# A hybrid attention and expert layer on one core: the first 512 value columns move from the projection slots into the opening sweep

## The reference, cut to what matters

```python
ada = silu(c) @ w_ada + b_ada                     # (1, 6 * 2048), w_ada 2048 x 12288
sh_m, sc_m, gt_m, sh_f, sc_f, gt_f = split(ada, 6)
h = rms_norm(x, g_pre_mix) * (1 + sc_m) + sh_m    # x: 256 tokens x 2048
proj = h @ w_in                                   # w_in 2048 x 6160
qa, ka, va, qb, kb, vb, rb, zb = split(proj)      # 1024, 1024, 1024, 512, 512, 1024, 1024, 16 columns
oa = diff_attention(qa, ka, va, rel_bias, lam)    # 8 heads, two softmax maps each, 2 blocks of 128 queries
ob = rms_norm(gla(qb, kb, vb, log_a(zb))) * silu(rb)
x = x + gt_m * rms_norm(concat(oa, ob) @ w_out, g_post_mix)
h = rms_norm(x, g_pre_ffn) * (1 + sc_f) + sh_f
x = x + gt_f * rms_norm(hier_moe(h), g_post_ffn)  # 32 experts, w1 and w3 2048 x 512, w2 512 x 2048 each
```

## Time and profile before

| | |
|---|---|
| median of 3 runs | 1465.71 us (1464.82 to 1466.46) |
| the profiled execution | 1463.97 us, of it span 1462.0 us |
| busy shares | TensorE 84%, VectorE 53%, ScalarE 14%, GpSimd 4% |
| chain that ended last | TensorE 45%, DMA 44%, VectorE 6% |
| moved | 583.5 MB, mean 399 GB/s |

### The profile page before, as it was taken

How to read it: one execution, slowest core, us unless ns; L and a number is a source line. 1 busy time by engine, 2 the same in 40 slices (tenths; PEclk the granted TensorE clock), 3 DMA queues, 4 the chain that set the end, 5 groups by cost and what they waited for, 6 DMA issues and landing times.

```text
span 1462.0 us, 18971 instructions
## 1 busy us (share of the span) xinstructions
PE 1221.2 (84%) x7437; PEld 575.1 (39%) x7438; DVE 778.9 (53%) x1110; ACT 211.7 (14%) x491; POOL 52.9 (4%) x68
## 2 busy tenths in 40 slices
PE   4699999999999989886777677758676679999967
PEld 4578884744444443222222222212222223333322
DVE  5877487877769666342234323422333335555525
ACT  3010121232110041010000000000000001111103
POOL 1000300011100020000000000000000000000020
PEclk9899999999999999988888889987888889999989
DMA  9999988797999899999999999999999999999996
GB/s 354 392 383 384 351 317 346 291 378 274 367 409 412 345 379 396 431 430 433 431 432 431 430 434 430 430 432 432 434 431 432 431 432 431 431 432 430 433 427 262
DMA packets 81557, 583.52 MB, mean 399 GB/s; under 512 B 5280, under 2 KB 30160, under 8 KB 56816
## 3 DMA queue, kind: packets, MB, share of 16 engines
q1 hardware_dynamic: 74160, 564.41, 93.6%
q10 hardware_dynamic: 5808, 14.85, 2.7%
q0 software_dynamic: 1552, 3.75, 0.8%
HBM read 579.30 MB, written 3.69 MB: 399 GB/s over the span
## 4 chain that ended last, share of the span: by engine, by line
PE 45%; DMA 44%; DVE 6%; SPq 2%; issue 1%; ACT 1%; POOL 0%; ACTq 0%; DVEq 0%
DMA stream<-in_w 41%; PE ps L1019 9%; PE ps L788 8%; PE ps L675 5%; PE ps L1075 4%; PE ps L740 3%; DMA stream<-in_w_ada 3%; PE ps L1026 2%; PE ps L975 2%; PE ps L878 2%; PE ps L969 2%; SPq L510 2%; PE ps L785 1%; DVE stream L1298 1%; DVE wk L1161 1%; DVE acc L1270 1%
## 5 line engine op out<-in xcount | busy, mean ns | idle before, releaser
L1019 PE MATMUL ps<-stream,wk 128*32 128x512 f32 x2304 | 330.2, 711 | 179.6 <-DMA stream<-in_w 178.9
L1536 DVE TENSOR_TENSOR acc<-ps,acc 128x2048 f32<-128x2048 f32 x37 | 84.8, 2292 | 364.4 <-PE ps L975 364.4
L1019 PEld LDWEIGHTS ps<-stream,wk 128*32 128x32 f32 x2304 | 74.7, 125 | 417.5 <-issue 332.5
L788 PE MATMUL ps<-stream 128*128 128x512 f32 x320 | 140.5, 593 | 0.1
L1075 PE MATMUL ps<-stream,cst 128*32 128x512 f32 x1152 | 131.5, 595 | 8.4 <-DMA stream<-in_w 8.4
L675 PE MATMUL ps<-stream 128*128 128x256 f32 x512 | 118.1, 394 | 1.8 <-ACT stream L1681 1.8
L675 PEld LDWEIGHTS ps<-stream 128*128 128x128 f32 x512 | 100.9, 198 | 16.8 <-issue 1.9
L1026 PEld LDWEIGHTS ps<-cst,wk 128*128 128x128 f32 x576 | 76.4, 207 | 69.0 <-issue 69.0
L975 PE MATMUL ps<-wk,cst 32*128 32x512 f32 x592 | 91.1, 687 | 0.8 <-ACT wk L1876 0.8
L1161 DVE SCALAR_TENSOR_TENSOR wk<-stream,cc,wk 128x768 f32<-128x768 f32 (+1 forms) x90 | 83.6, 929 | 11.0 <-DMA stream<-in_w_ada 8.3
L788 PEld LDWEIGHTS ps<-stream 128*128 128x128 f32 x320 | 59.5, 190 | 69.7 <-issue 69.7
(11 more groups left out here) (281 smaller groups left out, 1105.4 us busy)
## 6 DMA issues: line engine op xcount, KB each, us to landing
stream<-in_w SPq DMA_DIRECT2D x87, 4096.0 KB, 41.9
stream<-in_w_ada SPq DMA_DIRECT2D x64, 1024.0 KB, 8.8
stream<-in_w_in SPq DMA_DIRECT2D x8, 4096.0 KB, 16.5
stream<-in_w SPq DMA_DIRECT2D x16, 2048.0 KB, 11.7
stream<-in_w_ada SPq DMA_DIRECT2D x64, 384.0 KB, 10.1
stream<-in_w_ada SPq DMA_DIRECT2D x16, 512.0 KB, 9.7
stream<-in_w_in SPq DMA_DIRECT2D x4, 2048.0 KB, 13.7
stream<-in_w_out SPq DMA_DIRECT2D x2, 4096.0 KB, 16.4
```

What stands on the lines that cost most here:

```text
L788: last = nc.tensor.matmul(bank(fill % 2), hT[:, k, P * half:P * half + P], w[:, k, :], start=(k == 0), stop=(k == KD - 1))
L1019: last = nc.tensor.matmul(bank(1 + m)[32 * g:32 * g + 32, :], xe[:, k + g, :], w13[m][:, k + g, :], start=(k == 0), stop=(k == KD - 4))
L1536: V.tensor_tensor(y4, ps[:, b0:b0 + 4, :], y4, ALU.add).then_inc(ysum_sb, 1)
```

## The change

The opening sweep gets two more units, 8 and 9. Each is one block of 128 tokens (t = 0 or 1) by the 512 columns 2048 to 2559: one matmul of 512 columns for each k step, with `hT` as the stationary side and the weights as the moving side. They use bank 6 too, so four units share it (`SHARED = 4`), and the running sums of the two new ones lie in `acc`; the last stage's sum goes to `va`. The weights come in further slabs of 512 columns (rows of 2 KB), after the 2048 columns of the stage. Unit 4 is gone from the slots, with its load and its seven products; 28 slots remain, unit 5 is the only block unit, and attention starts at slot 4. `ADA_IN` is written anew: four slots take one load, 22 take two, two take none, and the four steps after them are as before. The row of the relative bias is computed ahead of the sweep's last unit, in bank 7, and its two tables are loaded ahead of GpSimd's other loads. The semaphore of the three small loads at the start is one with that of the constants.

```diff
-HEADS_READY = [8, 16]
+WIDE = 10
+SHARED = WIDE - 6
-TURN = [6, 0, 1, 2, 7, 3, 4, 5]
-SLOTS = 32
-BLOCK_UNITS = [4, 5]
+TURN = [6, 0, 7, 1, 8, 2, 3, 4, 9, 5]
+ADDED_AT = {8: {1: 6, 3: 7, 5: 8}, 4: {0: 6, 2: 7, 3: 8}}
+SLOTS = 28
+BLOCK_UNITS = [5]
-ATT_FROM = 6
-ADA_IN = [1, 1, 1, 1, 1, 1, 1, 1, 2, 2, 2, 2, 0, 2, 2, 1, 2, 2, 2, 1, 2, 2, 0, 2, 1, 2, 2, 2, 3, 2, 2, 0, 4, 5, 4, 3]
+ATT_FROM = 4
+ADA_IN = [1, 1, 1, 1, 2, 2, 2, 2, 2, 2, 0, 2, 2, 2, 2, 2, 2, 2, 2, 0, 2, 2, 2, 2, 2, 2, 2, 2, 4, 5, 4, 3]
...
+def wide_slabs(j):
+    lo, hi = STAGES[j]
+    cuts = [lo] + [k for k in range(lo + 1, hi) if k % HOMES in (0, 6)] + [hi]
+    return list(zip(cuts, cuts[1:]))
...
-    out = [(4 * i + 3.9, ("unit", i + 2)) for i in range(8)]
+    out = [(4 * i + 3.9, ("unit", i + 3)) for i in range(7)]
...
+        def wide_home(lo, hi):
+            r = lo % HOMES
+            return slab(s4, 4096 + 512 * r, hi - lo, 512) if r < 6 else slab(gl, 1920 + 512 * (r - 6), hi - lo, 512)
...
+                for a_, b_ in wide_slabs(j):
+                    if a_ == 6:
+                        sp.wait_ge(xT_ps, 4 * TT)
+                    sp.dma_start(wide_home(a_, b_), w_in[:, a_:b_, 256 * EARLY:256 * EARLY + 512]).then_inc(early_w_in[j % 3], 16)
...
-                    pe.wait_ge(add_sb, 2 * j + u - HELD)
+                    pe.wait_ge(add_sb, SHARED * j + u - HELD)
+                if u >= EARLY:
+                    t = u - EARLY
+                    for k in range(lo, hi):
+                        last = nc.tensor.matmul(bank(HELD), hT[:, k, P * t:P * t + P], wide_home(k, k + 1)[:, 0, :], start=(k == lo), stop=(k == hi - 1))
+                    last.then_inc(add_ps, 1)
+                    return last
...
-                    if n == EARLY - 2 and j + 1 < len(STAGES):
+                    if n == WIDE - 2 and j + 1 < len(STAGES):
                         early_sums(j + 1)
+                    if n == WIDE - 1 and j + 1 == len(STAGES):
+                        pe.wait_ge(tab_in, 16 * len(tables))
+                        pe.wait_ge(early_mod, len(STAGES))
+                        nc.tensor.matmul(bank(7)[:, 0:SKEW], relb, bkt[:, 0:SKEW], start=True, stop=True).then_inc(relrow_ps, 1)
...
-                    if j and n_ in (len(pieces(j)) // 4, 3 * len(pieces(j)) // 4):
-                        added(j - 1, HELD + n_ // (len(pieces(j)) // 2))
+                    if j and n_ in ADDED_AT[len(pieces(j))]:
+                        added(j - 1, ADDED_AT[len(pieces(j))][n_])
...
+                if j:
+                    added(j - 1, WIDE - 1)
```

More of the change, by code:

```diff
@@ L153, in schedule @@
     beside = [[] for _ in range(SLOTS)]
-    beside[0] += [("alpha", 0), ("row",)]
+    beside[0] += [("alpha", 0)]
     beside[1] += [("alpha", 1)]
@@ L157, in schedule @@
     beside[3] += [("lam",), ("tail", 0)]
-    beside[7] += [("tail", 1)]
-    beside[4].append(("alpha", 2))
+    beside[3].append(("alpha", 2))
     for m in (2, 3):
@@ L168, in schedule @@
         beside[ATT_FROM + j].append(("att", j))
-    beside[12].append(("kdec",))
-    beside[25].append(("kv", 0))
-    beside[26] += [("glao", 0), ("kv", 1)]
-    beside[27] += [("glao", 1), ("gsq", 0)]
-    beside[28] += [("gsq", 1)]
-    beside[29] += [("gmul", 0, 0), ("gmul", 1, 0)]
-    beside[30] += [("gmul", 0, 1)]
-    beside[31] += [("glaT", 0)]
+    beside[8].append(("kdec",))
+    beside[23].append(("kv", 0))
+    beside[24] += [("glao", 0), ("kv", 1)]
+    beside[25] += [("glao", 1), ("gsq", 0)]
+    beside[26] += [("gsq", 1), ("gmul", 0, 0)]
+    beside[27] += [("gmul", 1, 0), ("gmul", 0, 1), ("glaT", 0)]
     out = []
@@ L179, in schedule @@
         i, half, part = slot_unit(s)
-        out.append(("block", i - 4, 2 * half + part) if i in BLOCK_UNITS else ("proj", i, half, part))
+        out.append(("block", i - 5, 2 * half + part) if i in BLOCK_UNITS else ("proj", i, half, part))
         out += beside[s]
@@ L198, in loads @@
 def loads():
-    out = [(4 * i + 3.9, ("unit", i + 2)) for i in range(8)]
+    out = [(4 * i + 3.9, ("unit", i + 3)) for i in range(7)]
     out += [(max(ada_slot(n - 4) + 0.5, 1.9), ("ada", n)) for n in range(4, 64)]
-    return [("unit", 0), ("unit", 1), ("ada", 0), ("ada", 1), ("ada", 2), ("ada", 3)] + [item for _, item in sorted(out)]
+    return [("unit", 1), ("unit", 2), ("ada", 0), ("ada", 1), ("ada", 2), ("ada", 3)] + [item for _, item in sorted(out)]
 def build(nc, a, out):
@@ L380, in out_block @@
         def out_block(b, t, n):
[L382 removed]
+            return va[:, t, 512 + 256 * n:512 + 256 * n + 256]
         def block_bank(b, n):
[L386 removed]
+            return bank((6, 0, 1)[n % 3])[:, 0:256]
         hsum = [view(s3, 2048 + 1024 * i, 8, P) for i in range(4)]
@@ L709, in _ @@
                     fold(mod_bank(m)[:, 16 * m:16 * m + 16], 64).then_inc(mod_ps, 1)
-                elif kind == "row":
-                    nc.tensor.matmul(bank(4)[:, 0:SKEW], relb, bkt[:, 0:SKEW], start=True, stop=True).then_inc(relrow_ps, 1)
                 elif kind == "alpha":
@@ L781, in _ @@
                     elif part == 0:
-                        pe.wait_ge(blk_out, 8 * len(BLOCK_UNITS) - 1 + fill - HELD)
+                        pe.wait_ge(blk_out, 8 if fill > HELD else 4)
                     if c in TRANSPOSED:
@@ L1138, in added @@
             def added(j, u):
-                home = kaT[:, 2 * u - 8:2 * u - 6, :]
-                n = 2 * j + u - HELD
+                n = SHARED * j + u - HELD
+                if u < EARLY:
+                    home, src = kaT[:, 2 * u - 8:2 * u - 6, :], bank(HELD, 2, S)
+                else:
+                    home, src = acc[:, 512 * (u - EARLY):512 * (u - EARLY) + 512], bank(HELD)
+                to = va[:, u - EARLY, 0:512] if u >= EARLY and j + 1 == len(STAGES) else home
                 dve.wait_ge(add_ps, n + 1)
                 if j == 0:
-                    V.tensor_copy(home, bank(HELD, 2, S)).then_inc(add_sb, 1)
+                    V.tensor_copy(home, src).then_inc(add_sb, 1)
                 else:
                     dve.wait_ge(add_sb, n)
-                    V.tensor_tensor(home, bank(HELD, 2, S), home, ALU.add).then_inc(add_sb, 1)
+                    V.tensor_tensor(to, src, home, ALU.add).then_inc(add_sb, 1)
             def early(j):
@@ L1197, in _ @@
                 early(j)
-            for u in range(HELD, EARLY):
+            for u in range(HELD, WIDE - 1):
                 added(len(STAGES) - 1, u)
@@ L1684, in _ @@
             for u in range(HELD):
+                if u == HELD - 1:
+                    act.wait_ge(relrow_ps, 1)
+                    A(relrow, bank(7)[:, 0:SKEW], ACT.Copy).then_inc(relrow_sb, 1)
                 act.wait_ge(proj_ps, u + 1)
@@ L1702, in _ @@
                 kind = item[0]
-                if kind == "row":
-                    act.wait_ge(relrow_ps, 1)
-                    A(relrow, bank(4)[:, 0:SKEW], ACT.Copy).then_inc(relrow_sb, 1)
-                elif kind == "lam":
+                if kind == "lam":
                     act.wait_ge(lam_sum, 1)
@@ L1935, in _ @@
             pool.wait_ge(padded, 3)
+            for dst, src in tables:
+                pool.dma_start(dst, src).then_inc(tab_in, 16)
             for dst, src in params:
```

71 lines of the change are left out of this document (34 added, 37 removed).

## The result

| | before | changed |
|---|---|---|
| median of the runs shown together | 1466.09 us (4 runs, 1464.82 to 1467.61) | 1456.27 us (4 runs, 1454.26 to 1456.87) |
| ratio | | 0.9936, 95% interval 0.9923 to 0.9948 |
| measured again later | 1467.55 us (11 runs, 1463.02 to 1469.20) | 1457.90 us (6 runs, 1455.26 to 1460.10), ratio 0.9933 (0.9917 to 0.9949) |
| profiled execution | 1463.97 us, span 1462.0 | 1455.99 us, span 1454.1 |
| first block product | 165.34 | 182.95 |

The change is faster, by 0.64%. The forecast was 1457.3 us, with 0.80 on faster. The gain stands complete at the experts' first product (551.87 - 544.35 = 7.5 us) and the span has 7.9.

The account below looks back on a forecast made before the run. Loads were taken to bound the sweep, TensorE the slots, so work moves to where TensorE has room. Sweep +17.7, slots -24.5 and -0.9, w_out wait -0.7: total -8.4, 1457.3 us against the median 1465.71, range 1453.0 to 1464.4.

Parts of the forecast that it names:

- Sweep, +17.7: Opening sweep: with the two new units and the bias row it ends at 182.7, 17.7 us later than 165.0.
- There the loads set the cadence: Opening sweep: loads, not TensorE, set the 25.1 us stage; with the new bytes 27.1 us, fifth stage's fold at 132.6.
- Waits on the shared bank, 0: Sweep, bank shared by four units: TensorE waits for VectorE's additions add nothing, 1 us as the upper end.
- Sweep of TensorE, 26.5 a stage and 49.9 to the end: Sweep: TensorE's work is 26.5 us a stage, and 49.9 us from the fifth stage's fold to the sweep's end.
- rival 2: Sweep becomes bound by TensorE at a fallen clock: stage 28.0 us, gain only 4 to 5 us, 1461 us; chance 0.18.
- Slots, -24.5 and -0.9: Slots: unit 4's seven products go, -24.5 us; the bias row's 0.9 us leaves too, being counted in the sweep.
- Waits at L858, no change: Transposes in the slots (L831 before): one wait goes and one of the same size comes, 0, ends -1.8 and +5.
- step 5 about 1.8 us late: Slots: VectorE starts step 5 about 1.8 us late; before, late enough for the 1.8 us wait at L831.
- glaT, 2.7 us of room: Transposes of glaT after VectorE's last gmul: 2.7 us of room, so no wait there.
- After the slots, -0.7: TensorE's 3.0 us wait for a load of w_out (L920 before) shrinks by 0.7 us, ends -3 and 0.
- Rival 1: Loads become the bound in the slots if delivered below 348 GB/s: +5.6 us, 1471 us; chance 0.10.
- Rival 3: No change, 1465.5 us: w_out's loads come no earlier, or the shared bank costs 1.5 us each stage; together 0.10.

Follow-up runs that it names:

- The third experiment: Kernel before with four idle-filling matmuls of 384 columns ahead of each fold of stages 2 to 6: 1467.96 us, one run.
- the second experiment: Changed kernel with all loads kept, but units 8 and 9 multiply only 64 of their 512 columns: 1454.89 us, one run.
- The first: Changed kernel without the loads of the 512 new columns, units 8 and 9 multiplying columns already there: 1453.95 us, one run.
- the fifth experiment: Changed kernel with unit 7's partial sum added a piece earlier in the stages of four pieces: 1456.81 us, one run.
- the seventh experiment: Changed kernel with VectorE's multiply-adds evened out, slots 13 and 19 taking one load each instead of two and none: 1456.00 us, one run.
- the fourth experiment: Changed kernel with half the bytes in each of the 64 loads of 1 MiB: 1470.9 us, not comparable because the experts' choice changes.

## Why the prediction was right, and where it was not

The whole: -8.4 us forecast, -7.98 in the profiled executions, -9.8 between the medians. (The lower end of the range follows from -12.5 as 1453.2, not 1453.0.) By its terms:

1. **Sweep, +17.7**: measured 182.95 - 165.34 = +17.6. The sum was right by luck, for two of its steps were wrong and cancelled: the fifth stage's fold came 1.7 us sooner than the 132.6 forecast (130.94), and 1.3 us of waiting, forecast as nothing, came on top. "There the loads set the cadence" is the step that failed: the earlier trace rows had the wait of 1.01 us for unit 7 in it, and I read the 25.1 us as loads. The third experiment has 24.3 us for the same stage with the clock kept. The right sum for the loads was 24.3 + 2.0 = 26.3, and the second experiment measured 26.1 to 26.4. The slices of the earlier trace rows were read one too wide as well: the fifth is full, below full are slices 6, 7, 8, 10 and 14.
2. **Waits on the shared bank, 0**: measured 1.31 us, over the end of 1 that I gave. It is the other half of the same error. I had TensorE start its fifth stage at 132.6, in step with the loads. It started 1.7 us sooner, while VectorE's pieces came with the loads, so its addition, at an end of 148.16 against the 148.9 that the forecast implies, was 1.3 us late for unit 8. The first and the fifth experiment both take this wait away, one by earlier pieces, one by an earlier addition. The bank held TensorE in the first two stages as well (2.03, 1.10 and 0.80 us); those waits lie ahead of the fold at 130.94 and are in its place already.
3. **Sweep of TensorE, 26.5 a stage and 49.9 to the end**: from 130.94 to 158.76 are 27.8 us, 26.5 of them work; up to 182.65 it is 51.7, 50.4 without the wait. Right to half a microsecond. The stages of the changed kernel are as long as TensorE's work, and the loads need as long within 0.3 us; that was rival 2 without its price, for the clock did not fall.
4. **Slots, -24.5 and -0.9**: from the first product to glaT 253.87 us became 230.45, -23.4. Waits of 3.24 us instead of 1.8 account for 1.4 of the difference to 25.4; 0.5 us I cannot place. (Half of the 49.5 us of busy time is 24.75, not 24.5; from start to start a product takes 3.5 us, and seven of them 24.5.)
5. **Waits at L858, no change**: measured +1.4. The step of 128 to 256 keys was followed rightly to the second wait (VectorE 3.6 us late at step 9, 3.2 forecast), which the seventh experiment confirms as VectorE's own work. What failed is "step 5 about 1.8 us late": it was 3.9 us late, for I had followed VectorE's work alone, and its 2.20 us of waiting for a load at 232.5 was not in it, though the trace of the kernel before had such a wait, 1.73 us ahead of 245.72.
6. **glaT, 2.7 us of room**: no wait there, right; VectorE's last gmul ends at 410.81, 2.6 us ahead of 413.40. **After the slots, -0.7**: measured -1.4 at the wait; from w_out's first product to the experts' first 72.3 became 72.0 us.

Rival 1 (the loads bind the slots, 1471 us) needed less than 348 GB/s; 365 were delivered, and with 247 asked for, in the fourth experiment, line 892 came only 0.6 us sooner. The Trainium skill's 358 GB/s for a core (DMA: Bandwidth & Descriptors, section Where 436 GB/s comes from), named there beside it, is exceeded here by that 365 over 200 us. Rival 2 had the right binder and the wrong clock: with no idle time ahead of the folds the clock is 1.00 from 100 to 103. Rival 3 fell: w_out's wait halved, and the shared bank made TensorE wait 1.31 us in one of the last four stages, not in each.

## What to carry to other kernels

A stage that shows idle time on TensorE and a wait of VectorE for TensorE in the same stage may be bound by neither alone: before taking its length as that of the loads, look for what goes round through the clock (here 0.8 us of 25.1). Work moved into such idle time can cost less than its own length: here the 48 matmuls of 256 columns of a stage take 21.0 us at the kept clock where they took 22.55. A filler ahead of a fold that has no idle time only adds its length (2.7 us in the third experiment). And when a small gain upstream vanishes, look for a wait downstream that has become a little longer, and at the granted clock right behind it.
